# Six output blocks of a two-layer network multiplied by 64-row halves of TensorE's array

## The chip, the cores and the metric

The kernel runs on one core of a Trainium2 chip. The metric is the device time of the core in microseconds (us). TensorE's clock has two levels, 1.2 and 2.4 GHz; the profile gives the granted share of it. The profiled execution is one run of the same program under the hardware profiler.

## The reference

`reference()` sends one sequence of 256 tokens, 1024 wide, in fp32, through two layers, one after the other. What matters here are the three feed-forward parts, each followed by a residual addition:

```
u = square(relu(h @ w_up));       x = x + u @ w_down                       # 4096 hidden columns
u = silu(a) * b, a,b = h @ w_in;  x = x + 0.5 * g1 * (u @ ffn1_w_out)      # 2816 hidden columns
u = silu(a) * b, a,b = h @ w_in;  x = x + 0.5 * g3 * (u @ ffn2_w_out)      # 2816 hidden columns
```

The attention layers, the convolution and the recurrent part around them are not touched by the change.

## The kernel before, in words

**Blocks and units.** Every large product is cut into blocks: 256 tokens (two tiles `t` of 128) by 512 output columns. A block sums over the contraction dimension in chunks `k` of 128 rows. `down0` and `down1` are the two column halves of `u @ w_down` (32 chunks each); `ffn1o0`, `ffn1o1`, `ffn2o0`, `ffn2o1` are those of the two other output products (22 chunks each). A unit is two chunks of weights (512 KB); `half(u, t)` in the TensorE program (L1304 and after) is one unit for one token tile.

**Three products per chunk.** Weights and activations are split into a high part (type fp32r) and the remainder (fp32r as well). For each chunk and token tile TensorE makes three matrix multiplications into the same PSUM bank: high by high (L1320), high activations by low weights (L1324), low activations by high weights (L1325). Each has 128 rows of contraction, 128 stationary columns (tokens) and 512 moving columns (weights). A unit is so 12 multiplications. Plain fp32 operands are used elsewhere, in attention scores (L1415), which are already made in 64-row pairs, and in the recurrent part (L1547, L1548). For a plain fp32 matrix multiplication the trace records two instructions.

**Preparation.** SP loads a unit into one of four `raw` buffers. ACT makes the high part (`whi`, L1596), DVE the low part (`wlo`, L1984). There are five `whi`/`wlo` pairs, some more in a few stages. All engines run one written-out list, `order`, which `plan()` makes: each engine takes its own entries of it in order. Numbers in `LAG`, `ADA` and `LO` set how many steps a job waits.

**PSUM.** Eight banks: `pairs` is a ring of two pairs of banks, which the blocks use in turn; `misc` is a ring of four single banks, which transposes and attention use. A block in `pairs` takes one pair, one bank for each token tile.

**The end of a stage.** `residual(prefix, stage, ...)` runs `gemm` for column half 0, adds its two banks to `x` on DVE (`resid`: one addition at L2060 for `down`, or a multiplication by the gate at L2067 and an addition at L2071), then runs `gemm` for column half 1 with its last units left out (`leave`: 4 for `down1` and `ffn2o1`, 5 for `ffn1o1`), and `tail` runs the ones left out, first all for token tile 0, then all for tile 1, with the transposes of the next stage's input between them (L1351).

Of the kernel before, what the change touches and what calls it, by code (L numbers as in the profile page):

```python
# [16 lines left out]
OUTS = 2  # L17
LATE = NW + LENT
NEVER = (None, 0)
BEYOND = {"ffn2a0": ("ffn2b0", 1)}  # L20
BEHIND = {("up0", 3): 4, ("ffn1a0", 3): 4, ("ffn2a0", 3): 5, ("ffn2b0", 0): 3}

# [127 lines left out]
def build(nc, d, out):  # L150
# [5 lines left out]
    MUL, ADD, SUB = ALU.mult, ALU.add, ALU.subtract  # L156
# [7 lines left out]
    def signal(name, step=1):  # L164
        signals.append(Signal(ctx.enter_context(nc.semaphore(name)), step))
        return signals[-1]
# [6 lines left out]
    pairs = Ring([(ps[0], ps[1]), (ps[2], ps[3])])  # L173
    misc = Ring([ps[4], ps[5], ps[6], ps[7]])
# [11 lines left out]
    whi = [sb(f"whi{i}", [128, KU * 512], f32r) for i in range(NW)]  # L186
    wlo = [sb(f"wlo{i}", [128, KU * 512], f32r) for i in range(NW)]
    x = [sb(f"x{t}", [128, D]) for t in range(2)]
# [156 lines left out]
    def heads(v, h):  # L345
# [40 lines left out]
        signal(n) for n in ("lo_dve", "mean", "x_dve", "lower", "hn_mean", "hn_out", "swung"))  # L386
    cosed, turned_by, roped, p_max, p_mix, pt_dve, mixed_a = (
        signal(n) for n in ("cosed", "turned_by", "roped", "p_max", "p_mix", "pt_dve", "mixed_a"))
    tab8, consts, lam_sum, gate_turned, mod, scaled, x_new, gated = (
        signal(n) for n in ("tab8", "consts", "lam_sum", "gate_turned", "mod", "scaled", "x_new", "gated"))  # L390
    swapped, squared, glu, gate_in, gate_neg, gate_lf, gate_cum, gate_nat = (
        signal(n) for n in ("swapped", "squared", "glu", "gate_in", "gate_neg", "gate_lf", "gate_cum", "gate_nat"))
    conv_out, vm_put, s_decayed, h_put, fv_put, fox_in = (
# [75 lines left out]
    for u, (key, j) in lent.items():  # L469
        i = BEGIN.index(key)  # L470
        place[u], last_use[u] = NW + j, blocks[BEGIN[i - 1]]["units"][j] if i else None
        if key == "ffn2a0":
            place[u], last_use[u] = LATE + 1 + j, None

    DEFER = {blocks[key]["units"][j]: n for (key, j), n in BEHIND.items()}

    def last_half(key):
# [5 lines left out]
    def plan():  # L483
# [83 lines left out]
        def gemm(key, skip=0, leave=0):  # L567
            b = blocks[key]
            skip = max([skip, *(n for k, n in BEYOND.values() if k == key)])
            if b["pair"] == key and not skip:  # L570
                while None not in pairs.held:
                    tick()
                pairs.take(key)
            for u in b["units"][skip:len(b["units"]) - leave]:
                for t in range(2):
                    half(u, t)
                    paced(key)
# [195 lines left out]
        def resid(stage, key, c, gate, t, square=True):  # L773
            if gate:
                nat.take("res", stage, t, c)
                nat.drop("res", stage, t, c)
            order.append(("resid", stage, key, c, gate, t))
            if stage != "end" and square:
                square_of(stage, c, t)

        def square_of(stage, c, t):
            sqr.take("x", stage, t, c)
            sqr.drop("x", stage, t, c)
            order.append(("square", stage, c, t))
# [59 lines left out]
        def residual(prefix, stage, then=None, gate=False):  # L844
            gemm(f"{prefix}0")
            for t in range(2):
                resid(stage, f"{prefix}0", 0, gate, t)
            pairs.drop(f"{prefix}0")
            lead = lag(stage, "lead", LEAD)
            gemm(f"{prefix}1", leave=lead)  # L850
            if stage in FFN:
                ada_until(3 * FFN[stage] + 1)
                order.append(("mods", stage))
            tail(stage, [(f"{prefix}1", lead, 1)], then, gate)
# [340 lines left out]
    def left_ready(act, k, t):  # L1195
        p = k % 4 // 2
        if act == "mixT":
            return lower(f"ta{t}" if k < 4 else f"tb{t}")
        if act == "y":
            return lower("yT", k // 2)  # L1200
        if act == "yb":
            return lower(f"yb{k // 4}", p)
        if act == "merged":
            return lower(f"mT{k // 4}", p)
        if act[:2] == "u_":
            return lower(hidden(act, k), t)
        if act == "attn":
            return lower(act, k)
        return lower(act, t, 3 if k > 3 else k // 2)
# [24 lines left out]
    def uview(buf, u):  # L1234
        _, _, _, n, _, ncol = units[u]
        return buf[slot(buf, u)][:, 0:n * ncol].rearrange("p (k n) -> p k n", k=n)
# [31 lines left out]
        return mm(blocks[key]["units"][-1], t)  # L1268

    def pair_of(key):  # L1270
        return pairs.buf(blocks[key]["pair"])

    def attention(name):
        if name[:2] == "fx":
# [28 lines left out]
    def tensor_program(pe):  # L1303
        def half(u, t):  # L1304
            key, _, k0, n, _, ncol = units[u]
            b = blocks[key]
            h, l = uview(whi, u), uview(wlo, u)
            Ah, Al = LEFT[b["act"]]
            o = pair_of(key)[t][:, 0:ncol]
            if b["first"] and k0 == b["k0"]:  # L1310
                pe.wait_ge(*pairs.free(b["pair"], part=t))
            begin = key == "qa"
            pe.wait_ge(*(hi if begin else lo_dve)(u))
            for j in range(n):
                a = k0 + j + b["off"]
                pe.wait_ge(*(x_hi(a) if begin else left_ready(b["act"], a, t)))
                ah, al = Ah[:, a, t * 128:(t + 1) * 128], Al[:, a, t * 128:(t + 1) * 128]
                s0 = b["first"] and k0 + j == b["k0"]
                s1 = b["last"] and k0 + j == b["end"] - 1
                pe.e.matmul(o, ah, h[:, j, :], start=s0, stop=False, skip_group_check=True)  # L1320
                if begin:
                    pe.wait_ge(*lo_dve(u))
                    pe.wait_ge(*lower("attn", a))
                pe.e.matmul(o, ah, l[:, j, :], start=False, stop=False, skip_group_check=True)  # L1324
                r = pe.e.matmul(o, al, h[:, j, :], start=False, stop=s1, skip_group_check=True)  # L1325
            r.then_inc(mm.up(u, t), 1)

        def gate_mm(u):
            h, l, o = uview(whi, u), uview(wlo, u), pairs.buf("gate")[0][0:36, 0:256]
# [643 lines left out]
    def vector_program(dve):  # L1973
# [42 lines left out]
        def split(stage, t, p):  # L2016
            ts = slice(t * 128, (t + 1) * 128)
            buf = sqr.buf("n", stage, t, p)
            dve.wait_ge(*hT_free(stage, t))
            for c, n in ((0, 2), (2, 2)) if p == 0 else ((0, 4),):  # L2020
                k = 4 * p + c
                s = buf[:, c * 128:(c + n) * 128].rearrange("p (c t) -> p c t", c=n)
                dve.wait_ge(*n_scaled(stage, t, k + n - 1))
                step(v.tensor_copy(hTh[:, k:k + n, ts], s))
                dve.wait_ge(*dve_step.now())
                v.tensor_tensor(hTl[:, k:k + n, ts], s, hTh[:, k:k + n, ts].bitcast(f32), SUB).then_inc(
                    lower.up(stage, t, (k + n - 1) // 2), 1)
                sqr.give(lower(stage, t, (k + n - 1) // 2), "n", stage, t, p)
# [14 lines left out]
        def setup_lam():  # L2043
# [9 lines left out]
            v.tensor_scalar(lv, lv, -LI, None, ADD)  # L2053
            v.tensor_scalar(st(1, "sub c"), col("sub"), 1.0 - LI, None, MUL).then_inc(consts.up("sub"), 1)

        def residual(stage, key, c, gate, t):
            bank, xs = pair_of(key)[t], x[t][:, c * 512:(c + 1) * 512]
            dve.wait_ge(*mm(blocks[key]["units"][-1], t))
            if not gate:
                v.tensor_tensor(xs, xs, bank[:, :], ADD).then_inc(x_new.up(stage, t, c), 1)  # L2060
                r = x_new(stage, t, c)
            else:
                g = {"mix": 0, "ffn2": 1, "end": 0}[stage]
                nb = nat.buf("res", stage, t, c)
                dve.wait_ge(*nat.free("res", stage, t, c))
                dve.wait_ge(*ld_gate(g if stage != "end" else 2))
                v.tensor_tensor(nb[:, :], bank[:, :], gates[g][:, c * 512:(c + 1) * 512], MUL).then_inc(  # L2067
                    gated.up(stage, t, c), 1)
                r = gated(stage, t, c)
                dve.wait_ge(*r)  # L2070
                v.tensor_tensor(xs, xs, nb[:, :], ADD).then_inc(x_new.up(stage, t, c), 1)  # L2071
                nat.give(x_new(stage, t, c), "res", stage, t, c)
            pairs.give(r, blocks[key]["pair"], part=t)

        def gate(g, c):
            for t in range(2):
# [489 lines left out]
        for what, *of in order:  # L2566
            if what == "lo":
                prep(*of)
            elif what == "first_lo":
                first_lo(*of)  # L2570
            elif what == "job" and of[0] in jobs:
                next(jobs[of[0]], None)
            elif what == "mods":
                mods(*of)
            elif what == "scale":
                scale(*of)
            elif what == "split":
                split(*of)
            elif what == "resid":
                residual(*of)  # L2580
            elif what == "gate":
                gate(*of)
            elif what == "branch":
                branch(*of)
            elif what == "setup":
                setup(*of)
# [374 lines left out]
```

## Time and profile before

| what | value |
|---|---|
| three timed runs | 942.2, 942.33, 1035.65 us; median 942.33 |
| profiled execution, its own time | 943.64 us |
| its span in the trace | 942.3 us |
| TensorE matmul busy | 934.9 us of the span |
| weight loads busy | 772.2 us |
| VectorE busy | 718.1 us |
| ScalarE busy | 510.7 us |
| mean granted TensorE clock | 1.000 |

A busy share counts each instruction from its start to its modelled end, and matrix multiplications overlap: the time one of them costs in a dense stream is the distance from its start to the start of the next, not its own duration.

### The profile page before, as it was taken

The page shows a single profiled execution, that of the slowest core. Times are in us where ns is not written, and L with a number is a line of the kernel's source. Part 1 is how long each engine was busy: PE and PEld are TensorE (multiplying, and loading weights), DVE is VectorE, ACT ScalarE, POOL GpSimd, SP SyncE. Part 2 cuts the span into 40 slices and gives each one's busy share as a digit, 9 for nine tenths or more (in the row PEclk, how much of TensorE's full clock was granted, in tenths as well). Part 3 has the DMA queues.
Part 4 walks back from the last instruction along what each step waited for, and adds up shares of the span by engine and source line. Part 5 has one row for each costly group of instructions (what it writes and reads, how often), then busy time and mean ns, then how long its engine had stood idle before and what let it go on. Part 6 is the DMA issues. An engine that isn't in the chain of part 4 may idle for free.

```text
span 942.3 us, 12243 instructions
## 1 busy us (share of the span) xinstructions
PE 934.9 (99%) x4426; PEld 772.2 (82%) x4426; DVE 718.1 (76%) x1090; ACT 510.7 (54%) x792; POOL 50.5 (5%) x58
## 2 busy tenths in 40 slices
PE   9999999999999999999999999999999999999998
PEld 7878888888888888888888888878788888888886
DVE  6897689998776878777769999888667765566662
ACT  6686656554446445444576664456464574444440
POOL 2410000000000000000000121110000000000000
PEclk9999999999999999999999999999999999999999
DMA  9842579999894989998847889984735648666870
GB/s 343 263 159 83 179 261 369 401 383 362 283 322 145 341 325 345 323 348 278 275 134 260 288 271 292 300 330 148 232 125 190 211 137 260 228 224 223 297 238 23
DMA packets 123130, 240.31 MB, mean 255 GB/s; under 512 B 9346, under 2 KB 28954, under 8 KB 122814
## 3 DMA queue, kind: packets, MB, share of 16 engines
q1 hardware_dynamic: 122926, 239.27, 74.2%
q8 instruction: 35, 0.57, 0.3%
q10 hardware_dynamic: 144, 0.27, 0.1%
q14 instruction: 25, 0.20, 0.1%
HBM read 226.35 MB, written 14.20 MB: 255 GB/s over the span
## 4 chain that ended last, share of the span: by engine, by line
PE 96%; DMA 1%; DVE 1%; POOL 0%; issue 0%; ACT 0%; DVEq 0%
PE ps L1320 30%; PE ps L1324 29%; PE ps L1325 29%; PE ps L1459 2%; DMA raw<-in_w_mix 1%; PE ps L1415 1%; PE ps L1440 1%; PE ps L1373 1%; PE ps L1351 1%; PE ps L1572 1%; POOL stat L2595 0%; DVE stat L2193 0%; PE ps L1474 0%; DVE over L2225 0%; PE ps L1493 0%
## 5 line engine op out<-in xcount | busy, mean ns | idle before, releaser
L1596 ACT ACTIVATE whi<-raw 128x1024 fp32r<-128x1024 f32 (+1 forms) x285 | 294.7, 1046 | 272.0 <-PE ps L1325 176.8
L1984 DVE TENSOR_TENSOR wlo<-raw,whi 128x1024 fp32r<-128x1024 f32 (+1 forms) x285 | 338.6, 1204 | 104.6 <-ACT whi L1596 104.1
L1320 PE MATMUL ps<-whi,hTh 128*128 128x512 f32 (+1 forms) x760 | 299.9, 395 | 0.0
L1324 PE MATMUL ps<-wlo,hTh 128*128 128x512 f32 (+1 forms) x760 | 294.4, 387 | 0.1
L1325 PE MATMUL ps<-whi,hTl 128*128 128x512 f32 (+1 forms) x760 | 294.4, 387 | 0.0
L1320 PEld LDWEIGHTS ps<-whi,hTh 128*128 128x128 f32 x760 | 142.8, 188 | 30.6 <-issue 2.5
L1325 PEld LDWEIGHTS ps<-whi,hTl 128*128 128x128 f32 x760 | 142.7, 188 | 29.5
L1324 PEld LDWEIGHTS ps<-wlo,hTh 128*128 128x128 f32 x760 | 142.9, 188 | 28.1 <-issue 0.4
L2326 DVE CUSTOM_DVE_ANT_0 araw<-araw,crow,colp 128x1024 f32<-128x1024 f32 x72 | 92.0, 1278 | 0.4 <-DMA araw<-in_w_mod 0.4
L2595 POOL TENSOR_TENSOR stat<-stat,mhalf 128x8 f32<-128x8 f32 (+3 forms) x29 | 36.9, 1284 | 584.4 <-DVE stat L2000 458.4
L1320 PE MATMUL ps<-whi,uh_ffn 128*128 128x512 f32 x164 | 63.9, 390 | 0.0
L1324 PE MATMUL ps<-wlo,uh_ffn 128*128 128x512 f32 x164 | 63.8, 389 | 0.0
L1325 PE MATMUL ps<-whi,ul_ffn 128*128 128x512 f32 x164 | 63.8, 389 | 0.0
L1320 PE MATMUL ps<-whi,uh 128*128 128x512 f32 x128 | 49.9, 390 | 0.0
L1325 PE MATMUL ps<-whi,ul 128*128 128x512 f32 x128 | 49.8, 389 | 0.0
L1324 PE MATMUL ps<-wlo,uh 128*128 128x512 f32 x128 | 49.8, 389 | 0.0
L2375 DVE TENSOR_TENSOR nat<-ps,nat 128x512 f32<-128x512 f32 (+1 forms) x24 | 15.3, 646 | 29.9 <-PE ps L1325 22.1
L1320 PEld LDWEIGHTS ps<-whi,uh_ffn 128*128 128x128 f32 x164 | 30.8, 188 | 6.4
L1325 PEld LDWEIGHTS ps<-whi,ul_ffn 128*128 128x128 f32 x164 | 30.8, 188 | 6.4
L1324 PEld LDWEIGHTS ps<-wlo,uh_ffn 128*128 128x128 f32 x164 | 30.8, 188 | 6.3
L1320 PEld LDWEIGHTS ps<-whi,uh 128*128 128x128 f32 x128 | 24.0, 188 | 5.0
L1324 PEld LDWEIGHTS ps<-wlo,uh 128*128 128x128 f32 x128 | 24.0, 188 | 5.0
(276 smaller groups left out, 1129.2 us busy)
## 6 DMA issues: line engine op xcount, KB each, us to landing
raw<-in_ffn_w_in SPq DMA_DIRECT2D x80, 512.0 KB, 5.3
araw<-in_w_mod SPq DMA_DIRECT2D x72, 512.0 KB, 5.7
raw<-in_w_mix SPq DMA_DIRECT2D x64, 512.0 KB, 5.1
raw<-in_ffn_w_out SPq DMA_DIRECT2D x44, 512.0 KB, 5.1
raw<-in_w_up SPq DMA_DIRECT2D x32, 512.0 KB, 5.5
raw<-in_w_down SPq DMA_DIRECT2D x32, 512.0 KB, 5.3
scr_u<-blocked SPq DMA_DIRECT2D x18, 512.0 KB, 4.8
raw<-in_w_out SPq DMA_DIRECT2D x16, 512.0 KB, 4.4
```

Of the source, the lines that this page charges most:

```text
L1320: pe.e.matmul(o, ah, h[:, j, :], start=s0, stop=False, skip_group_check=True)
L1324: pe.e.matmul(o, ah, l[:, j, :], start=False, stop=False, skip_group_check=True)
L1325: r = pe.e.matmul(o, al, h[:, j, :], start=False, stop=s1, skip_group_check=True)
L1351: r = pe.e.transpose(bank[:, c * 128:(c + 1) * 128], src[:, (4 * p + c) * 128:(4 * p + c + 1) * 128], ident[:, :])
L1373: r = pe.e.transpose(bank[:, c * 256 + t * 128:c * 256 + t * 128 + 128], src[t][:, (2 * p + c) * 128:(2 * p + c + 1) * 128], ident[:, :])
L1415: return pe.e.matmul(bank[:, c * w:(c + 1) * w], Q[rows, hp + c, ts], K[rows, kc(c), 0:w], start=True, stop=True)
L1459: r = pe.e.matmul(ob[:, h * 64:(h + 1) * 64], buf[:, (nk * c + k) * 128:(nk * c + k + 1) * 128], (fV if a["fox"] else VA)[:, k, v0:v0 + 64 ...
L1596: act.e.activation(uflat(whi, u), uflat(raw, u), ACT.Copy).then_inc(hi.up(u), 1)
L1984: v.tensor_tensor(uflat(wlo, u), uflat(raw, u), uflat(whi, u).bitcast(f32), SUB).then_inc(lo_dve.up(u), 1)
L2326: v.tensor_tensor_reduce(out=w, in0=w, in1=crow[:, :], scale=1.0, scalar=col("bada", 8 * m + i), op0=MUL, op1=ADD, accum_out=to).then_inc( ...
L2375: v.tensor_tensor(b[:, 0:n], pair_of(key)[t][:, c:512], b[:, 0:n], MUL).then_inc(glu.up(name, t), 1)
L2595: g.tensor_tensor(o, a, mhalf[:, 0:n], ALU.pow).then_inc(rstd.up(*key), 1)
```

## The change

In the six blocks named in `BY_ROWS` every multiplication of 128 contraction rows becomes two of 64 rows each: rows 0 to 63 of the array for the lower half of the operands, rows 64 to 127 for the upper half. The two write to different PSUM banks, so a block needs four banks: column half 0 takes the four `misc` banks, column half 1 takes both pairs of `pairs`. After the last unit of a by-rows stretch DVE adds the banks of the upper rows to `x` on their own (`fold`), for `ffn1` and `ffn2` after multiplying by the gate; `residual` then adds the lower rows' banks, as before. The units that `tail` runs (the last 4, 5 and 4 of the three blocks of column half 1) stay as they were, with full 128-row multiplications into the lower pair.

```
+BY_ROWS = ("down0", "down1", "ffn1o0", "ffn1o1", "ffn2o0", "ffn2o1")
...
         def gemm(key, skip=0, leave=0):
...
-            if b["pair"] == key and not skip:
+            if key in BY_ROWS:
+                ring, n = (misc, 4) if key[-1] == "0" else (pairs, 2)
+                while ring.held.count(None) < n:
+                    tick()
+                for i in range(n):
+                    ring.take(key, *(("row", i) if ring is misc else ("up",) * i))
+            elif b["pair"] == key and not skip:
...
+                if key in BY_ROWS:
+                    halved[u] = u == b["units"][-1 - leave]
...
         def residual(prefix, stage, then=None, gate=False):
             gemm(f"{prefix}0")
             for t in range(2):
+                fold(stage, f"{prefix}0", 0, gate, t)
                 resid(stage, f"{prefix}0", 0, gate, t)
-            pairs.drop(f"{prefix}0")
+            for i in range(4):
+                misc.drop(f"{prefix}0", "row", i)
             lead = lag(stage, "lead", LEAD)
             gemm(f"{prefix}1", leave=lead)
+            for t in range(2):
+                fold(stage, f"{prefix}1", 1, gate, t)
+            pairs.drop(f"{prefix}1", "up")
...
+        def half_by_rows(u, t):
+            key, _, k0, n, _, ncol = units[u]
+            b = blocks[key]
+            h, l = uview(whi, u), uview(wlo, u)
+            Ah, Al = LEFT[b["act"]]
+            o = pair_of(key)[t][:, 0:ncol], upper_rows(key)[t][:, 0:ncol]
+            if k0 == b["k0"]:
+                for token in row_banks_free(key, t):
+                    pe.wait_ge(*token)
+            pe.wait_ge(*lo_dve(u))
+            for j in range(n):
+                a = k0 + j + b["off"]
+                pe.wait_ge(*left_ready(b["act"], a, t))
+                begin, end = k0 + j == b["k0"], halved[u] and j == n - 1
+                for A, w, first, last in ((Ah, h, True, False), (Ah, l, False, False), (Al, h, False, True)):
+                    r = [pe.e.matmul(o[i], A[64 * i:64 * i + 64, a, t * 128:(t + 1) * 128], w[64 * i:64 * i + 64, j, :],
+                                     start=begin and first, stop=end and last, skip_group_check=True) for i in range(2)]
+            r[0].then_inc(mm.up("lower rows", u, t), 1)
+            r[1].then_inc(mm.up(u, t), 1)
...
+        def fold(stage, key, c, gate, t):
+            bank, xs = upper_rows(key)[t], x[t][:, c * 512:(c + 1) * 512]
+            last = max(u for u in blocks[key]["units"] if u in halved)
+            dve.wait_ge(*mm(last, t))
+            if gate:
+                g = {"mix": 0, "end": 0}[stage]
+                nb = nat.buf("fold", stage, t, c)
+                dve.wait_ge(*nat.free("fold", stage, t, c))
+                dve.wait_ge(*ld_gate(g if stage != "end" else 2))
+                v.tensor_tensor(nb[:, :], bank[:, :], gates[g][:, c * 512:(c + 1) * 512], MUL).then_inc(
+                    gated.up("fold", stage, t, c), 1)
+                r = gated("fold", stage, t, c)
+                dve.wait_ge(*r)
+                v.tensor_tensor(xs, xs, nb[:, :], ADD).then_inc(folded.up(stage, t, c), 1)
+                nat.give(folded(stage, t, c), "fold", stage, t, c)
+            else:
+                v.tensor_tensor(xs, xs, bank[:, :], ADD).then_inc(folded.up(stage, t, c), 1)
+                r = folded(stage, t, c)
```

## Rows read from the trace of the kernel before

**Rows 1.** The page: busy time by engine, and the chain that ended last.

```profile
PE 934.9 (99%) x4426; PEld 772.2 (82%) x4426; DVE 718.1 (76%) x1090; ACT 510.7 (54%) x792; POOL 50.5 (5%) x58
...
PE 96%; DMA 1%; DVE 1%; POOL 0%; issue 0%; ACT 0%; DVEq 0%
```

**Rows 2.** Stretches: from:to, length, busy by engine (instructions), clock, DMA share, GB/s.

```profile
201.00:274.00 73.00, 73.00 (x323) 60.44 (x322) 58.30 (x72) 33.57 (x38) 0.00 (x0) 1.00 0.94 331
...
409.00:451.00 42.00, 42.00 (x187) 34.79 (x186) 32.80 (x42) 19.46 (x25) 0.00 (x0) 1.00 0.88 308
...
875.00:915.00 40.00, 40.00 (x178) 33.14 (x177) 24.53 (x28) 18.24 (x22) 0.00 (x0) 1.00 0.84 278
```

**Rows 3.** Groups of TensorE by line and form: count | busy us, mean ns.

```profile
L1320 PE MATMUL ps<-whi,uh_ffn 128*128 128x512 f32 x164 | 63.9, 390 | 0.0
...
L1320 PE MATMUL ps<-whi,uh 128*128 128x512 f32 x128 | 49.9, 390 | 0.0
```

**Rows 4.** Timeline of TensorE inside down1: start us, duration us, instruction; ten in all.

```profile
261.76 0.39 PE L1320 MATMUL ps<-whi,uh 128*128 128x512 f32 x1
...
263.80 0.39 PE L1320 MATMUL ps<-whi,uh 128*128 128x512 f32 x1
```

**Rows 5.** Timeline of the weight loads in the same stretch; nine in all.

```profile
261.99 0.19 PEld L1325 LDWEIGHTS ps<-whi,ul 128*128 128x128 f32 x1
```

**Rows 6.** Timeline of TensorE at the recurrent part: plain fp32 on 128 rows.

```profile
559.26 0.59 PE L1547 MATMUL ps<-Vm,fP 128*128 128x257 f32 x2
559.69 0.60 PE L1548 MATMUL ps<-Vm,fP 128*128 128x257 f32 x2
```

**Rows 7.** Timeline of TensorE around two runs of attention scores in 64-row pairs.

```profile
53.38 0.40 PE L1325 MATMUL ps<-whi,hTl 128*128 128x512 f32 x1
53.71 2.00 PE L1415 MATMUL ps<-kbT,qbT 64*128 64x256 f32 x16
55.64 0.50 PE L1320 MATMUL ps<-whi,hTh 128*128 128x512 f32 x1
55.98 0.40 PE L1324 MATMUL ps<-wlo,hTh 128*128 128x512 f32 x1
...
58.74 0.39 PE L1325 MATMUL ps<-whi,hTl 128*128 128x512 f32 x1
59.06 1.13 PE L1415 MATMUL ps<-kbT,qbT 64*128 64x256 f32 x8
60.12 0.50 PE L1320 MATMUL ps<-whi,hTh 128*128 128x512 f32 x1
60.46 0.40 PE L1324 MATMUL ps<-wlo,hTh 128*128 128x512 f32 x1
```

**Rows 8.** The start of the first of these runs, cut off at 53.75 us.

```profile
53.71 0.19 PEld L1415 LDWEIGHTS ps<-kbT,qbT 64*128 64x128 f32 x2 [0.36 <-issue]
53.71 0.49 PE L1415 MATMUL ps<-kbT,qbT 64*128 64x256 f32 x2
```

**Rows 9.** Timeline of TensorE: fp32r by 256 columns, with 128 and with 36 stationary columns.

```profile
45.46 0.28 PE L1324 MATMUL ps<-wlo,hTh 128*128 128x256 f32 x1
...
45.94 0.28 PE L1325 MATMUL ps<-whi,hTl 128*128 128x256 f32 x1
...
484.18 0.28 PE L1335 MATMUL ps<-hTh,whi 128*36 128x256 f32 x1
...
484.86 0.28 PE L1335 MATMUL ps<-hTh,whi 128*36 128x256 f32 x1
```

**Rows 10.** Waits and DVE groups of the output stages, 201:290 and 409:480 us.

```profile
ACT whi L1596 <- PE ps L1325: 37.9, 25, 1.7
...
L2060 DVE TENSOR_TENSOR x<-x,ps 128x512 f32<-128x512 f32 x4 | 2.6, 682 | 0.8 <-PE ps L1325 0.8
...
L2071 DVE TENSOR_TENSOR x<-x,nat 128x512 f32<-128x512 f32 x4 | 2.8, 692 | 0.1
L2067 DVE TENSOR_TENSOR nat<-ps,gate 128x512 f32<-128x512 f32 x4 | 2.7, 687 | 0.3 <-PE ps L1325 0.3
```

More of the change, by code:

```diff
@@ L388, in build @@
         signal(n) for n in ("cosed", "turned_by", "roped", "p_max", "p_mix", "pt_dve", "mixed_a"))
-    tab8, consts, lam_sum, gate_turned, mod, scaled, x_new, gated = (
-        signal(n) for n in ("tab8", "consts", "lam_sum", "gate_turned", "mod", "scaled", "x_new", "gated"))
+    tab8, consts, lam_sum, gate_turned, mod, scaled, x_new, gated, folded = (
+        signal(n) for n in ("tab8", "consts", "lam_sum", "gate_turned", "mod", "scaled", "x_new", "gated", "folded"))
     swapped, squared, glu, gate_in, gate_neg, gate_lf, gate_cum, gate_nat = (
@@ L473, in build @@
             place[u], last_use[u] = LATE + 1 + j, None
+    halved = {}
     DEFER = {blocks[key]["units"][j]: n for (key, j), n in BEHIND.items()}
@@ L779, in resid @@
                 square_of(stage, c, t)
+        def fold(stage, key, c, gate, t):
+            if gate:
+                nat.take("fold", stage, t, c)
+                nat.drop("fold", stage, t, c)
+            order.append(("fold", stage, key, c, gate, t))
         def square_of(stage, c, t):
@@ L1270, in pair_of, with upper_rows, row_banks_free @@
     def pair_of(key):
+        if key in BY_ROWS and key[-1] == "0":
+            return [misc.buf(key, "row", t) for t in range(2)]
         return pairs.buf(blocks[key]["pair"])
+    def upper_rows(key):
+        return [misc.buf(key, "row", 2 + t) for t in range(2)] if key[-1] == "0" else pairs.buf(key, "up")
+    def row_banks_free(key, t):
+        if key[-1] == "0":
+            return misc.free(key, "row", t), misc.free(key, "row", 2 + t)
+        return pairs.free(key, part=t), pairs.free(key, "up", part=t)
     def attention(name):
@@ L1309, in half @@
             o = pair_of(key)[t][:, 0:ncol]
+            if u in halved:
+                half_by_rows(u, t)
+                return
             if b["first"] and k0 == b["k0"]:
@@ L2054, in setup_lam, with fold @@
             v.tensor_scalar(st(1, "sub c"), col("sub"), 1.0 - LI, None, MUL).then_inc(consts.up("sub"), 1)
+        def fold(stage, key, c, gate, t):
+            bank, xs = upper_rows(key)[t], x[t][:, c * 512:(c + 1) * 512]
+            last = max(u for u in blocks[key]["units"] if u in halved)
+            dve.wait_ge(*mm(last, t))
+            if gate:
+                g = {"mix": 0, "end": 0}[stage]
[11 more added lines that the diff above has]
+                r = folded(stage, t, c)
+            if c:
+                pairs.give(r, key, "up", part=t)
+            else:
+                misc.give(r, key, "row", 2 + t)
         def residual(stage, key, c, gate, t):
@@ L2059, in residual @@
             if not gate:
+                if key in BY_ROWS:
+                    dve.wait_ge(*folded(stage, t, c))
                 v.tensor_tensor(xs, xs, bank[:, :], ADD).then_inc(x_new.up(stage, t, c), 1)
@@ L2070, in residual @@
                 dve.wait_ge(*r)
+                if key in BY_ROWS:
+                    dve.wait_ge(*folded(stage, t, c))
                 v.tensor_tensor(xs, xs, nb[:, :], ADD).then_inc(x_new.up(stage, t, c), 1)
                 nat.give(x_new(stage, t, c), "res", stage, t, c)
-            pairs.give(r, blocks[key]["pair"], part=t)
+            if key in BY_ROWS and key[-1] == "0":
+                misc.give(r, key, "row", t)
+            else:
+                pairs.give(r, blocks[key]["pair"], part=t)
         def gate(g, c):
@@ L2578, in vector_program @@
                 split(*of)
+            elif what == "fold":
+                fold(*of)
             elif what == "resid":
```

## The prediction, made before the changed kernel was built or run

> **What bounds the kernel now.** The page comes first [rows 1]. TensorE is busy 934.9 of 942.3 us, and the chain that ended last runs through it for 96%. Only what shortens or lengthens TensorE's own stream moves the time. The stretches of the three output stages confirm it where the change works: TensorE is busy all of the 73, 42 and 40 us, DVE 58.3, 32.8 and 24.5 us, all at a granted clock of 1.00, that is at 2.4 GHz [rows 2]. The preparation runs ahead: in 201 to 290 us ACT waited 25 times, 37.9 us in all, for TensorE to free a buffer [rows 10], and TensorE waited for nobody.
>
> Then the step of the stream, from start to start. In down1 nine steps take 263.80 - 261.76 = 2.04 us, 0.2267 us each [rows 4]. The duration column (0.39) overlaps and is not the cost. At 2.4 GHz 0.2267 us are 544 columns for 512 moved: 32, or 13.3 ns, are lost in each. The weight load is no reason for it at first sight: it takes 0.19 us and starts with the multiplication before it [rows 5].
>
> **How many multiplications change.** The high by high group of down has 128, that of ffn has 164 and some more under another buffer's name [rows 3]; by the block sizes each down block has 32 chunks x 2 tiles x 3 = 192, each ffn output block 22 x 2 x 3 = 132, together 912. The tails keep 4, 5 and 4 units of 12, so 156. Changed are 756; each becomes a pair.
>
> **What a pair costs.** The trace has 64-row pairs only in plain fp32: the scores. There 16 recorded instructions of 256 columns take, from the start of the run to the next full-array instruction, 55.64 - 53.71 = 1.93 us, and 8 take 60.12 - 59.06 = 1.06 [rows 7]. The difference, 0.87 us for 4 pairs, is 0.217 us a pair. Two of them start within the same 0.04 us, and so do their two weight loads [rows 8]. The same plain instruction on all 128 rows, with 257 columns, takes 0.43 us for two, 0.215 each [rows 6]. I read two things there. The halves do run side by side, weight loads included. And a pair costs what one full instruction of the same type costs, no more and no less: in plain fp32 both are at the step that is short by those 32 columns. So the loss of 13.3 ns belongs to fp32r, not to the full array.
>
> Is it something that half the rows would remove? Rows with fp32r at 256 columns speak to that. With 128 stationary columns four steps take 45.94 - 45.46 = 0.48 us, 0.120 each, which is 106.7 ns of streaming (256 at 2.4 GHz) and again 13.3. With 36 stationary columns six steps take 484.86 - 484.18 = 0.68 us, 0.113 each [rows 9], with 6.7 ns left over. Both have 128 rows. The loss goes with the stationary columns, and the change leaves these at 128 in each half. Between the bounds (213.3 ns, pure streaming, 10.1 us less over 756; and 453 ns, two halves one after the other) I take the value of the nearest row of the same type, 227 ns a pair: **0 us**.
>
> The Trainium skill speaks against the change here. "TensorE: Matmul & The Clock Gate", Part 3, models side-by-side tiles as the duration of one multiplication plus about 4 ns for each further tile; the gain it promises is for contractions that leave rows idle, and here none do. Were that 4 ns paid by every pair, the sum would grow by 3.0 us. The score pairs, at 0.217 against 0.215, neither show it nor exclude half of it.
>
> **Switching between full and half array.** Around the long run of scores, from the L1325 before it to the L1324 after: 55.98 - 53.38 = 2.60 us, against 0.227 + 8 x 0.216 + 0.227 = 2.18; around the short one 60.46 - 58.74 = 1.72 against 1.32 [rows 7]. A round trip costs 0.40 to 0.42 us whatever lies inside. No transposes and no other full-array work falls within the changed part of a stage, so there are three round trips (down, ffn1, ffn2): **+1.2 us**, on TensorE and so on the path. "TensorEngine Tiling (Array Packing)", Key Properties, in the Trainium skill says that a change of tiling mode drains the engine; the 0.41 us agree.
>
> **The folds on DVE.** Four folds for down (one addition, 682 ns) and eight for the ffn stages (687 + 692 ns) [rows 10]: 4 x 0.68 + 8 x 1.38 = 13.8 us more on DVE, none at the very end, since the folds of the last block come with 4 units still to run. The worst place is the end of ffn1o0 and ffn2o0: a fold and a residual for each tile, 5.5 us in a row on an engine whose queue then holds the next low parts. Five weight buffers are prepared ahead, and the four behind the current one last 4 x 12 x 0.2267 = 10.9 us, so TensorE does not notice: **0 us**. Uncovered it would be at most the 13.8. Where the folds would be felt first is in down, where DVE has 14.7 us of 73 free [rows 2].
>
> **Banks, buffers, order.** Column half 0 no longer waits for a pair but for four single banks, which nobody else uses in these stages; column half 1 needs both pairs, and the former block's pair is read some 40 us earlier. The following stage's first block takes down1's lower pair instead of the other one; token tile 0 of it was added to x 5 us before. Doubled instructions of TensorE (about 1500 multiplications and as many loads more) come at four for each pair, 57 ns each; the score run had 32 in 1.93 us, 60 ns each. SP's transfers are the same in number and size. **0 us**, with 1 us either way for the shifted order.
>
> **Sum.** The profiled execution's own time is 943.64 us (span 942.3 and 1.3 around it), 1.31 above the median of 942.33. 943.64 + 1.2 = 944.8, on the median's scale **943.5 us**.
>
> **The rivals.**
>
> *The loss of fp32r goes away in halves* (chance 0.34). Pairs then run at the 0.216 of the score pairs: 756 x 10.7 ns = 8.1 us less, 1.2 more for the switches: 935.4 us; with pure streaming 10.1 less, 933.4. For it: the only pairs in the trace have that step, and why 32 columns are lost is shown by no row. Against: plain fp32 has it without halves. The Trainium skill's "TensorE: Matmul & The Clock Gate", Back-to-back issue gap, gives columns over 2.4 GHz plus 2.5 ns, 215.8 for 512, without naming fp32r; by that figure the sum would be this rival's.
>
> *The weight loads of the two halves hold each other's stream* (0.09). If the 32 lost columns come from the load, and both loads of a pair stop both streams, a pair is at 240 ns: 756 x 13.3 = 10.1 us more, 953.6. Against: two loads in plain fp32 cost nothing visible.
>
> *The halves are not side by side in fp32r, or not fed fast enough* (0.15). The place is the pair in each half(u, t): 2 x 0.2267 for each, 756 x 0.2267 = 171 us more, 1115 us in the full case, which would also mean that the change doesn't do what it says. It decides for "slower by over 2%" from (18.8 - 1.2)/756 = 23 ns a pair, that is from a step of 250 ns, or 62.5 ns for each of the four instructions. For it: no row has fp32r on half rows, and no row has more than 32 instructions at such a rate. Against: plain fp32 does both.
>
> **How the numbers follow.** The forecast has 0.42; its own range is 941 to 947. The range goes from 933.4, the lower end of the first rival, to 955, past the second; left out is the third. A difference of 2%, 18.8 us, is about what a measurement of this kernel can tell from no change. No case reaches it on the fast side, since a pair cannot stream in less than 213.3 ns; faster 0.01. The first two rivals and the forecast lie within 2%: 0.84. Slower: 0.15.
>
> **What would show it.** In down1 of the changed kernel the start of one pair to the next: 227 ns (forecast), 216 (first rival), 240, or above 250. The two instructions of a pair start within 10 ns. A step of 0.33 us where a stage enters the halves. DVE about 14 us busier, TensorE waiting for it nowhere. Wrong it is if the step is not 227, or if TensorE idles before the first unit after a fold.

## The result and the profile after

The changed kernel takes 947.5 us (median of 4, 946.08 to 947.7) against 942.28 for the kernel before: ratio 1.0047, 95% interval 1.0035 to 1.006. One of the four executions of the kernel before took 1035.65 us, the other three 942.2 to 942.33, and the ratio goes without it. The medians are 5.2 us apart, where 1.2 were forecast. (Their quotient would be 1.0055; the ratio is estimated otherwise, and its interval stands for 3.3 to 5.7 us.) The profiled execution took 947.42 us with a span of 946.1.

The page, busy time and chain, the same view as [rows 1]:

```profile
PE 936.1 (99%) x5182; PEld 772.4 (82%) x5182; DVE 731.8 (77%) x1110; ACT 509.9 (54%) x792; POOL 49.6 (5%) x58
...
PE 96%; DVE 2%; DMA 1%; issue 0%; ACT 0%; POOL 0%; DVEq 0%
```

TensorE has 756 instructions more, as counted. DVE is 13.7 us busier, 13.8 were forecast. DVE now has 2% of the chain, where it had 1%.

The pairs come first. The timeline of TensorE inside down0, the same view as [rows 4], two instructions of 64 rows on each line:

```profile
230.23 0.39 PE L1377 MATMUL ps<-whi,uh 64*128 64x512 f32 x2
...
232.27 0.39 PE L1377 MATMUL ps<-whi,uh 64*128 64x512 f32 x2
```

Nine pairs take 2.04 us, 0.2267 each: the step of the full array to the nanosecond. The halves run side by side and gain nothing. The entry into the halves and the way back to the full array, the same view as [rows 7]:

```profile
200.52 0.39 PE L1359 MATMUL ps<-whi,hTl 128*128 128x512 f32 x1
200.84 0.50 PE L1377 MATMUL ps<-whi,uh 64*128 64x512 f32 x2
201.17 0.40 PE L1377 MATMUL ps<-wlo,uh 64*128 64x512 f32 x2
...
203.26 0.39 PE L1377 MATMUL ps<-wlo,uh 64*128 64x512 f32 x2
...
276.92 0.39 PE L1377 MATMUL ps<-whi,ul 64*128 64x512 f32 x2
277.24 0.50 PE L1354 MATMUL ps<-whi,uh 128*128 128x512 f32 x1
277.58 0.40 PE L1358 MATMUL ps<-wlo,uh 128*128 128x512 f32 x1
```

The steps are 0.32 and 0.33 us going in, 0.32 and 0.34 coming out, against 0.227: 0.1 us each, 0.4 for a round trip. The nine steps behind them are a little long as well: 203.26 - 201.17 = 2.09 us, where nine steps of 0.2267 are 2.04. That is 0.05 us more. A switch so costs 0.25 us, a round trip 0.5, the three of them 1.5 us.

What the forecast did not have stands in the tail of ffn1. TensorE's waits in 440 to 480 us (who waited for whom: us in total, times, longest):

```profile
PE ps L1354 <- DVE wlo L2038: 2.2, 1, 2.2
PE ps L1405 <- DVE W L2062: 1.2, 1, 1.2
```

The kernel before has neither. DVE in the same place:

```profile
458.49 1.23 DVE L2038 TENSOR_TENSOR wlo<-raw,whi 128x1024 fp32r<-128x1024 f32 x1 [1.72 <-ACT whi L1650]
459.63 1.28 DVE L2410 CUSTOM_DVE_ANT_0 araw<-araw,crow,colp 128x1024 f32<-128x1024 f32 x1
...
460.84 0.69 DVE L2119 TENSOR_TENSOR nat<-ps,gate 128x512 f32<-128x512 f32 x1
461.56 0.69 DVE L2123 TENSOR_TENSOR x<-x,nat 128x512 f32<-128x512 f32 x1
462.17 0.69 DVE L2119 TENSOR_TENSOR nat<-ps,gate 128x512 f32<-128x512 f32 x1
462.89 0.69 DVE L2123 TENSOR_TENSOR x<-x,nat 128x512 f32<-128x512 f32 x1
463.50 0.16 DVE L2048 SCALAR_TENSOR_TENSOR sc<-modc,colp 128x8 f32<-128x8 f32 x1
463.57 1.22 DVE L2038 TENSOR_TENSOR wlo<-raw,whi 128x1024 fp32r<-128x1024 f32 x1
464.71 3.49 DVE L2038 TENSOR_TENSOR lent_lo<-raw,lent_hi 128x1024 fp32r<-128x1024 f32 x3
468.12 0.69 DVE L2146 TENSOR_TENSOR nat<-ps,gate 128x512 f32<-128x512 f32 x1
```

The four instructions from 460.84 are the folds of ffn1o1. The low part at 463.57 is that of the last unit of ffn1o1; TensorE starts on it at 464.85. Then the low parts of three units of the next stage stand before the residual of token tile 0 (468.12), on which the norm and the transposes depend: the second wait.

The high part for that unit was late as well. ACT's timeline in the kernel before, then in the changed one:

```profile
443.97 0.63 ACT L1602 ACTIVATE sq<-x 128x512 f32<-128x512 f32 x1 [0.60 <-DVE x L2071]
...
444.60 2.94 ACT L1596 ACTIVATE whi<-raw 128x1024 fp32r<-128x1024 f32 x3
...
456.80 1.06 ACT L1596 ACTIVATE whi<-raw 128x1024 fp32r<-128x1024 f32 x1 [1.66 <-PE ps L1325]
```

```profile
446.89 0.63 ACT L1656 ACTIVATE sq<-x 128x512 f32<-128x512 f32 x1 [1.93 <-DVE x L2152]
...
447.51 3.89 ACT L1650 ACTIVATE whi<-raw 128x1024 fp32r<-128x1024 f32 x4
453.37 1.06 ACT L1650 ACTIVATE whi<-raw 128x1024 fp32r<-128x1024 f32 x1 [1.96 <-DMA raw<-in_ffn_w_out]
457.40 1.06 ACT L1650 ACTIVATE whi<-raw 128x1024 fp32r<-128x1024 f32 x1 [2.97 <-DMA raw<-in_ffn_w_out]
459.98 1.07 ACT L1650 ACTIVATE whi<-raw 128x1024 fp32r<-128x1024 f32 x1 [1.52 <-DMA raw<-in_ffn_w_out]
```

SP's reloads of the raw buffers, before and after:

```profile
446.93 1.50 SPq L2693 DMA_DIRECT2D raw<-in_ffn_w_out  x2
```

```profile
449.85 1.50 SPq L2779 DMA_DIRECT2D raw<-in_ffn_w_out  x2
```

The folds of ffn1o0 make x complete later. ACT's squares of x wait for it, and the high parts of the next units stand behind the squares: they start at 447.51 instead of 444.60. The low parts follow, and SP reloads a raw buffer only after its low part, at 449.85 us instead of 446.93. From there on ACT waits for transfers, 6.5 us in three waits, where before it waited for TensorE; the last high part of ffn1o1 comes at 459.98 instead of 456.80.

### The profile page after: what moved, and what is told of

Read it like the earlier page. It is cut to its first block, busy times and chain, and to the rows that moved or that the text cites. A ratio compares the mean times of both kernels' runs of the same rounds, so it can differ in the third digit from the quotient of the medians.

```text
span 946.1 us, 13785 instructions
## 1 busy us (share of the span) xinstructions
PE 936.1 (99%) x5182; PEld 772.4 (82%) x5182; DVE 731.8 (77%) x1110; ACT 509.9 (54%) x792; POOL 49.6 (5%) x58
## 4 chain that ended last, share of the span: by engine, by line
PE 96%; DVE 2%; DMA 1%; issue 0%; ACT 0%; POOL 0%; DVEq 0%
PE ps L1354 24%; PE ps L1359 23%; PE ps L1358 23%; PE ps L1377 17%; PE ps L1513 2%; PE ps L1469 1%; PE ps L1427 1%; PE ps L1494 1%; PE ps L1405 1%; DMA raw<-in_ffn_w_out 1%; PE ps L1626 1%; DVE wlo L2038 1%; DVE lent_lo L2038 0%; DVE stat L2277 0%; ACT whi L1650 0%
## 5 line engine op out<-in xcount | busy, mean ns | idle before, releaser
L1377 PE MATMUL ps<-whi,uh_ffn 64*128 64x512 f32 x256 | 50.2, 389 | 0.0
L1377 PE MATMUL ps<-whi,ul_ffn 64*128 64x512 f32 x256 | 50.0, 387 | 0.0
L1377 PE MATMUL ps<-wlo,uh_ffn 64*128 64x512 f32 x256 | 49.9, 387 | 0.0
L1377 PE MATMUL ps<-whi,uh 64*128 64x512 f32 x224 | 43.8, 388 | 0.0
L1377 PE MATMUL ps<-whi,ul 64*128 64x512 f32 x224 | 43.8, 387 | 0.0
L1377 PE MATMUL ps<-wlo,uh 64*128 64x512 f32 x224 | 43.6, 387 | 0.0
L1377 PEld LDWEIGHTS ps<-whi,uh_ffn 64*128 64x128 f32 x256 | 24.0, 184 | 5.6 <-issue 0.7
L1377 PEld LDWEIGHTS ps<-wlo,uh_ffn 64*128 64x128 f32 x256 | 24.1, 185 | 4.9
L1377 PEld LDWEIGHTS ps<-whi,ul_ffn 64*128 64x128 f32 x256 | 24.1, 184 | 5.0
L2429 DVE STREAM_TRANSPOSE blocked<-nat 128x512 f32<-128x512 f32 (+1 forms) x40 | 24.9, 660 | 0.0
```

The costliest lines, as they stand in the source:

```text
L1377: r = [pe.e.matmul(o[i], A[64 * i:64 * i + 64, a, t * 128:(t + 1) * 128], w[64 * i:64 * i + 64, j, :], start=begin and first, stop=end and ...
L2429: v.transpose(blocked[:, 0:2 * n].rearrange("p (b t x) -> p t b x", b=4, t=2)[:, t], nat.buf(name, t)[:, 0:n].rearrange("p (b x) -> p b x" ...
```

## The experiments

The times of whole kernels are medians of 5 to 12 executions. The kernel before ran beside them on the same chip. It had 942.53 us in the first group (after_again, full_banks, no_folds, late_folds), 942.6 in the second (no_fold_mix0, no_fold_mix1, not_ffn1, both_orders), 942.57 in the third (before_again) and 942.35 in the last (three_orders). Differences to the changed kernel are to the 947.75 us of the first group.

**The changed kernel once more** (after_again). 

> The changed kernel once more, as the yardstick of this group. Theory (three switches between full and half array, 1.2 us, and about 3.6 us of TensorE idle in the tail of ffn1 because DVE is late with the folds, part of it made up later): 947.5 us, with one idle of 2.2 us before the last unit of ffn1o1 and one of 1.2 us before the transposes, in every execution. Rival (the excess over the forecast is an accident of one execution): nearer to 943.5 us.

947.75 us, ratio 1.0052 (1.004 to 1.0065), the same two waits of 2.2 and 1.2 us. The rival falls: the excess is not the accident of one execution.

**Four banks and folds, but no halves** (full_banks).

```
...
+                begin, end, i = k0 + j - b["k0"] < 2, halved[u] and j >= n - 2, (k0 + j) % 2
...
-                    r = [pe.e.matmul(o[i], A[64 * i:64 * i + 64, a, t * 128:(t + 1) * 128], w[64 * i:64 * i + 64, j, :],
-                                     start=begin and first, stop=end and last, skip_group_check=True) for i in range(2)]
...
+                    r = pe.e.matmul(o[i], A[:, a, t * 128:(t + 1) * 128], w[:, j, :], start=begin and first,
+                                    stop=end and last, skip_group_check=True)
...
```

Even chunks (`i` = 0) go to the lower bank, odd chunks to the upper one.

> The four banks and all twelve folds stay, but every chunk is multiplied on all 128 rows: even chunks into the lower banks, odd ones into the upper banks. No half-array pair is left. Theory (folds are the larger part, switches 1.2 us): the changed kernel less 1.2, that is 946.3 us, with the two idles in the tail of ffn1 still there. Rival (the halves themselves, their doubled instructions or their switches, cost the 5.2 us): 942.3 us.

945.38 us, ratio 1.0026 (1.0015 to 1.0038): 2.4 us less than with halves, not 1.2. The waits in the tail are still there, but smaller:

```profile
PE ps L1405 <- DVE W L2062: 1.4, 1, 1.4
PE ps L1354 <- DVE wlo L2038: 0.7, 1, 0.7
```

So the four banks and the folds cost 2.9 us without any half, and the rival falls. In the profiles 1.5 us less are the switches and 1.4 less the waits (4.0 and 2.6 in the table below); waits elsewhere hide a part of it. The first wait is shorter because the high part before last started at 454.70 us and not at 457.40, and DVE was through with the folds 2.7 us earlier (at 460.84 and not at 463.50).

**No folds** (no_folds). `fold` on DVE only gives the banks back; the kernel leaves out the upper rows' part of x.

> The halves stay, the twelve folds are left out, so that the upper rows' part of the six blocks is missing from x. Theory (only the three switches are left): 943.5 us, no idle of TensorE in the tail of ffn1. Rival (the halves and the changed bank order cost it): 947 us.

944.57 us, ratio 1.0019 (1.001 to 1.0028), no wait in the tail of ffn1: 3.2 us less than the changed kernel. The 1.2 us of the theory lie within the interval (0.9 to 2.6), in its lower part, and so do the 1.5 that the switches take.

**One pair of folds left out at a time.** The names are those of the runs: mix0 is ffn1o0, mix1 is ffn1o1. Each kernel leaves out the upper rows' part of its block.

> The changed kernel without the two folds of ffn1o0 alone (the upper rows' part of that block is missing from x). Theory (two blocks of folds add up: those of ffn1o0 hold back the squares on ACT, with them the preparation and the reloads of the raw buffers; those of ffn1o1 stand before the last low part): the transfers come in time again, the idle before the last unit of ffn1o1 goes, about 1.3 us is left before the transposes: 2.3 to 3 us less than the changed kernel, some 945 us. Rival (only the folds of ffn1o1 matter, since they stand right before the low part that TensorE waits for): 947.5 us.

> The changed kernel without the two folds of ffn1o1 alone (the upper rows' part of that block is missing from x). Theory (two blocks of folds add up): the idle before the last unit goes, but the late transfers still make the lent units' low parts late, and with them the residual and the transposes; the idle moves there: 947 us. Rival (only the folds of ffn1o1 matter): both idles go, 944 us.

Without those of ffn1o0: 945.52 us, ratio 1.0027 (1.0017 to 1.0037); one wait of 0.7 us before the transposes is left, ACT's waits for transfers fall from 6.5 to 3.3 us. Without those of ffn1o1, the ones directly before the low part: 947.8 us, ratio 1.0049 (1.0036 to 1.0061), nothing gained. The theory has both numbers right. The folds that stood next to the stall in the trace were not the ones whose removal shortens the run. But the second number is right in part by luck. Here is TensorE's timeline in that kernel, then stretches before, in and behind a slow part (from:to, length, busy by engine, then clock, DMA share, GB/s):

```profile
470.02 1.06 PE L1405 MATMUL ps<-ident,W 128*128 128x128 f32 x8 [1.99 <-DVE W L2062]
470.83 0.63 PE L1354 MATMUL ps<-whi,uh_ffn 128*128 128x512 f32 x1
471.26 0.63 PE L1358 MATMUL ps<-wlo,uh_ffn 128*128 128x512 f32 x1
```

```profile
466.00:469.90 3.90, 2.03 (x9) 1.33 (x8) 2.38 (x5) 1.24 (x3) 0.55 (x1) 1.00 0.92 266
471.00:474.30 3.30, 3.30 (x10) 2.53 (x9) 2.48 (x5) 2.84 (x9) 0.00 (x0) 0.50 0.25 44
475.00:478.00 3.00, 3.00 (x14) 2.25 (x12) 2.46 (x5) 0.72 (x2) 0.00 (x0) 1.00 0.09 34
```

The two waits, 2.2 and 1.2 us, have become one of 2.0 before the transposes, as expected. So leaving out the late folds does shorten the idle, by 1.4 us. But behind it the granted clock is 0.50, that is 1.2 GHz: eight steps take 0.43 us instead of 0.227, 1.6 us more, and the gain is gone. No expectation had that. It is not one execution either: the mean clock of its six executions was 0.998 in five and 0.999 in one; of the changed kernel's nine it was 0.998 in two, 0.999 in one and 1.000 in six.

**Halves in down and ffn2 only** (not_ffn1). `BY_ROWS` without the two ffn1 blocks, folds and drops made conditional on it.

> The halves and folds in down and ffn2 alone, ffn1 as before the change. Theory (ffn1 is the only stage in which the folds reach TensorE): two switches, 0.8 us, and no idle: 943.4 us. Rival (every stage has its part of the 5.2 us, by what the halves do elsewhere): 2/3 of it, 946 us.

944.54 us, ratio 1.002 (1.0011 to 1.0028), 3.2 us less than the changed kernel. So most of the excess belongs to ffn1; 0.5 of the 3.2 us are ffn1's own two switches. It is 1.9 above the kernel before, though, not 0.8. The four switches that are left make 1.0 of it. And TensorE still waits 0.8 us before the transposes of ffn1, with no fold in that stage: some wait there does not come from folds.

**The same work in another order.** Three kernels keep all of the change's work and move entries of the written-out order in ffn1:

```
     plan()
+    # late_folds
+    moved(fold t=0 of ffn1o1, behind low part 160); moved(fold t=1, behind the square of tile 0)
+    moved(low parts 161, 162, 163, behind scale of tile 0)
+    # both_orders
+    moved(squares of column half 0, behind high part 157); moved(fold t=1 of ffn1o1, behind low part 160)
+    # three_orders
+    moved(squares of column half 0, behind high part 157)
+    moved(low part 163, behind scale of tile 0); moved(fold t=1 of ffn1o1, behind scale of tile 0)
```

The last unit of ffn1o1 is 160; 161 to 163 are the lent units of the next stage.

> The changed kernel with DVE's order altered in the tail of ffn1 alone: the low part of the last unit of ffn1o1 comes first, then the fold of token tile 0; the fold of tile 1 stands behind the residual of tile 0, and the low parts of the three lent units behind the norm's scale. Same work. Theory (the idle is a matter of which DVE entry stands before the low part that TensorE needs next): the 2.2 us idle goes, at most 1 us is left before the transposes, 944.5 us. Rival (DVE or the transfers are simply out of time there, wherever the folds stand): the idle moves to the transposes and the time stays at 947.5 us.

946.63 us, ratio 1.0042 (1.0029 to 1.0054). The wait before the last unit is gone, but a new one of 1.4 us stands at the next stage's first units, whose activations' low parts (hTl) DVE makes behind the three moved ones. The idle moved on by one place. The time lies between theory and rival, nearer to the rival.

> The changed kernel, all its work kept, with two entries of the order altered in ffn1: ACT makes the squares of column half 0 four units later, behind the high parts of the next units, and DVE makes the fold of token tile 1 of ffn1o1 behind the low part of the last unit. Theory (the squares carry the folds' delay on to ACT and to the transfers): ACT no longer waits 6 us for transfers in that stretch, the idle of TensorE in the tail falls from 3.6 to 1 us or less: 944.5 to 945 us. Rival (DVE's added work alone makes it late): 947 us.

945.7 us, ratio 1.0031 (1.0022 to 1.004), between the two. The first wait is gone, 1.6 us before the transposes are left, and ACT still waits 4.1 us for transfers, so that part of the theory was too simple. The likely reason is that DVE's own delay also holds the reloads back; no run takes it alone.

> The changed kernel, all its work kept, with entries of the order altered in ffn1: the squares of column half 0 four units later; the fold of token tile 1 of ffn1o1 and the low part of the third lent unit behind the norm's scale of tile 0, so that they no longer stand before the residual of tile 0. Theory (what reached TensorE of the folds is their place in DVE's and ACT's queues): at most 0.7 us of TensorE idle in the tail of ffn1, 944 to 944.5 us, what the kernel without folds has. Rival (13.8 us more work on DVE has to show): 945.7 us as with the squares moved alone, or more.

944.69 us, ratio 1.0026 (1.0015 to 1.0038): 3.1 us less than the changed kernel, the same as without any fold. TensorE's only wait in 400 to 500 us, and DVE at the residual:

```profile
PE ps L1363 <- DVE hTl L2089: 0.3, 1, 0.3
```

```profile
464.08 0.69 DVE L2155 TENSOR_TENSOR nat<-ps,gate 128x512 f32<-128x512 f32 x1 [0.51 <-PE ps L1368]
464.81 0.69 DVE L2161 TENSOR_TENSOR x<-x,nat 128x512 f32<-128x512 f32 x1
...
467.57 0.68 DVE L2128 TENSOR_TENSOR nat<-ps,gate 128x512 f32<-128x512 f32 x1
```

The residual of tile 0 now waits for TensorE, at 464.08, and not for DVE's queue as at 468.12; the fold comes at 467.57, when nobody needs DVE. So 13.8 us more work on DVE hardly show, if they stand in the right place. The kernel is still not faster than the one before.

**The loss of fp32r by itself.** Two programs of their own with runs of 24 multiplications, each executed once. In short, with `c` stationary and `n` moving columns:

```
for k in range(24):
    pe.matmul(ps[1][0:c, 0:n], r[:, 512 + 128*(k%4) : 512 + 128*(k%4) + c], r[:, 0:n], ...)     # r: fp32r, b: bf16
```

> A program of its own that computes nothing of the reference: after 96 bf16 multiplications of 512 columns come runs of 24, back to back and each with its weight load: fp32r by 512 moving columns with 128, 96, 64 and 32 stationary columns on all 128 rows, plain fp32 by 256 columns, then 24 pairs of 64 rows with 128 stationary columns and 24 pairs with 64, and fp32r with the same stationary operand each time. Theory (the loss of fp32r over pure streaming, 213.3 ns, goes with the stationary columns, a fourth of a column's time for each, and not with the rows): steps of 226.7, 223.3, 220 and 216.7 ns, pairs at 226.7 and 220 ns, the last run at 226.7. Rival (the loss is one of the rows, or a fixed one of fp32r): 226.7 for all four, or pairs below 226.7 with 128 stationary columns.

> A second program of its own, runs of 24 as in the first: fp32r by 512 columns with 128 and 36 stationary columns, by 384 and 256 with 128, by 256 with 64 and 36 and again 128, by 512 into two banks in turn; 64-row fp32r pairs by 256; bf16 by 512 with 128 and 36 stationary columns, and bf16 pairs of 64 rows. Theory (after the first such program: the loss of fp32r over streaming is fixed, 13 to 17 ns a step, whatever columns, rows and banks): about 227 to 231, 227 to 231, 173, 120, 120, 120, 120, 227, 120 ns; bf16 216, 216 and pairs at 216. Rival (it does hang on the stationary columns at 256 moving columns, as the gate's rows of 113 ns in the kernel before had it): 120, 113 and 110 ns for 128, 64 and 36.

The lines of the first, then of the second; 24 steps are about the start of the next line less this one's:

```profile
33.72 5.69 PE L40 MATMUL ps<-r 128*96 128x512 f32 x24
39.25 5.68 PE L42 MATMUL ps<-r 128*64 128x512 f32 x24
44.76 5.72 PE L44 MATMUL ps<-r 128*32 128x512 f32 x24
50.33 10.52 PE L46 MATMUL ps<-r 128*128 128x256 f32 x48
60.78 5.76 PE L50 MATMUL ps<-r 64*128 64x512 f32 x48
66.37 5.69 PE L54 MATMUL ps<-r 64*64 64x512 f32 x48
```

```profile
34.20 5.60 PE L40 MATMUL ps<-r 128*36 128x512 f32 x24
39.64 4.35 PE L42 MATMUL ps<-r 128*128 128x384 f32 x24
...
43.83 3.03 PE L44 MATMUL ps<-r 128*128 128x256 f32 x24
46.69 2.89 PE L46 MATMUL ps<-r 128*64 128x256 f32 x24
49.42 2.97 PE L48 MATMUL ps<-r 128*36 128x256 f32 x24
...
74.29 5.35 PE L64 MATMUL ps<-b 64*128 64x512 bf16 x48
```

At 512 columns the step lies between 0.227 and 0.232 us for 36, 32, 64, 96 and 128 stationary columns: (39.64 - 34.20)/24 = 0.227 with 36, (39.25 - 33.72)/24 = 0.230 with 96, (50.33 - 44.76)/24 = 0.232 with 32. Fewer columns are not faster. The 24 pairs of 64 rows take (66.37 - 60.78)/24 = 0.233, but that holds the slow steps behind the switch; the last 15 are at 0.227. Pairs of bf16 take 0.216, as bf16 and plain fp32 do on the full array (all three by the last 15 steps). The first theory falls: at 512 columns the loss does not go with the stationary columns. It comes with the type fp32r, in all seven shapes tried. At 256 columns it is 13 ns with 128 stationary columns and 7 with 64 (0.120 and 0.114), but 0.117 with 36; the rival of the second program has the first two and not the third. Why fp32r loses them stays open.

**The kernel before once more** (before_again). 

> The kernel before once more, for a second profile beside its times. Theory (the small wait before the transposes of ffn1 varies from execution to execution, 0.2 to 1 us): the steps of 227 ns and the stages stand as in the first profile, with TensorE's waits within 1 us of it. Rival (the first profile is typical to the last wait): the same 0.16 us before the transposes at the end of ffn1.

942.8 us against 942.57 beside it, ratio 0.9998 (0.9986 to 1.001), span 940.6 in this profile against 942.3 in the first, no wait at all in the tail of ffn1. The rival falls. Two profiles of one kernel differ by 1.7 us here, so two spans alone do not place a difference of 1 us. But all these kernels send TensorE the same 4426 recorded multiplications in the same order, if a pair is counted once. So each profile can be laid beside this second one step by step, and every step that is longer is found. In us:

| profile | longer than before_again | switches | waits from the tail of ffn1 to the next stage's first units, with the slower steps behind them | elsewhere |
|---|---|---|---|---|
| after | 5.5 | 1.5 | 4.0 | 0.0 |
| full_banks | 3.3 | 0 | 2.6 | 0.7 |
| no_folds | 3.7 | 1.5 | 0.0 | 2.2 |
| no_fold_mix0 | 2.5 | 1.5 | 1.0 | 0.0 |
| no_fold_mix1 | 5.3 | 1.5 | 3.8 | 0.0 |
| not_ffn1 | 2.6 | 1.0 | 1.0 | 0.6 |
| three_orders | 2.4 | 1.5 | 0.8 | 0.1 |
| before | 1.7 | 0 | 0.2 | 1.5 |

What stands under "elsewhere" comes and goes. In four of these profiles, the kernel before among them, 0.4 to 0.9 us of it is one wait of TensorE for ACT, before a transpose near 624 us. In that of no_folds, the slowest of its 11 executions, 1.8 us lie in the first 100 us, where the granted clock is 0.50 from 73.2 to 76.5 us.

## Why the prediction was right, and where it was not

- **The pair costs 227 ns: right.** It was the step on which the case turned. The loss of fp32r stays in halves; the rival with 935 us, the one with loads that hold both streams and the one without overlap are all out by the pair's own rows, in down0 and through the other five blocks.
- **But the reason given was wrong.** "The loss goes with the stationary columns" was read from the gate's rows of 256 moving columns [rows 9] and carried to 512. The two programs show that it does not hold there. What held was the choice of the nearest row, the one of the same type. No row before the change showed that halves keep the loss, and the prediction gave 0.34 to their losing it: that the value came out exactly owes something to luck.
- **Three round trips, 1.2 us: right in kind and number, small in size.** They take 0.5 us each, 1.5 in all. The rows of the score runs [rows 7] were read up to the second step behind the run, and the nine slower steps after that were not counted. The kernels without most of the folds' waits stand 1.9 to 2.3 us above the kernel before (944.54 to 944.69 against 942.35 to 942.6). The table places that: 1.0 or 1.5 for the switches, 0.8 to 1.0 for a wait that is left at the end of ffn1 in two of the three, and waits elsewhere that the kernel before has at times too.
- **The folds, 0 us: the step that failed.** The two waits take 4.0 us of the changed kernel's profile. Without the folds the kernel is 3.2 us faster, with their order changed 3.1; with ffn1 left as before it is 3.2, of which 0.5 are switches. The prediction's own sign of being wrong, TensorE idle before a unit behind a fold, is what the trace shows, and 947.5 us lie just above the forecast's own range of 941 to 947 (the wide range, 933.4 to 955, holds them). The size on DVE was right (13.7 against 13.8). The cover was not. I took five buffers to last 10.9 us. In the tail the same units are run through for token tile 0 alone, each half in 1.36 us, so the last of the five is needed 4 x 1.36 = 5.4 us after the first. And I followed the folds on DVE only, not on to the squares in ACT's queue, the high parts behind them and the reloads that wait for the low parts. The prediction saw that the low parts are queued behind the folds; it did not ask who is queued behind the squares.
- **Where they would be felt first: wrong.** Down showed nothing, it was ffn1. The rows had a sign of it: in ffn1 DVE has 9.2 of 42 us free [rows 2] and the folds take 5.5, in down it has 14.7 of 73 and they take 2.7. ffn2 has neither squares nor a next stage. Which of these differences decides was not tested.
- **Banks, order, instruction rate: right.** Pairs keep their step through 336 of them in a row; no wait at the banks.

The sum as measured: 1.5 for the switches and 4.0 for the two waits in ffn1 make the 5.5 us between two profiles; the medians are 5.2 apart.

## What to carry to other kernels

Splitting full-array products into halves of the array gives no time back when all rows are in use: here a pair cost a full step, and each stretch a switch of 0.25 us on either side. Before an added instruction is called hidden, count the cover in the place where it is shortest (here a tail that uses every buffer for half a unit only) and follow the delay through every queue that waits for it, one engine after the other, until somebody has slack. When a stall shows up, the work right before it need not be its only cause: remove each suspect alone, and look at the idle time and the clock as well as at the time. Here the early folds' removal saved 2.2 us; the late ones' saved idle time, and the lower clock behind the idle took it back. And when two kernels run an engine through the same sequence, lay the two traces side by side step by step before a remainder is called open.

## What the runs showed of the hardware

- fp32r multiplications of 512 moving columns take 227 ns a step with 128 and with 36 stationary columns, and 230 to 232 with 96, 64 and 32; bf16 and plain fp32 of the same streaming time take 216 (plain fp32 counted by recorded instruction of 256 columns). Pairs of 64 rows with 128 stationary columns take the same 227 and 216. At 256 moving columns 128, 64 and 36 stationary columns gave 120, 114 and 117 ns.
- Two 64-row fp32r halves start 2 to 5 ns apart and run side by side for 336 pairs with no loss of rate: four instructions, two multiplications and two weight loads, every 227 ns.
- A switch between full array and halves in fp32r costs 0.25 us: two steps of 0.32 and 0.33 to 0.34 us, then nine of 0.232 on average.
- After an idle of 2.0 us TensorE made eight steps at a granted clock of 0.50 (0.43 us each). After idles of 2.2 and then 1.2 us in the changed kernel's profile it made none.
